# Masked level copies over the second halves only, and a ScalarE eviction moved behind the gate's first output

## The chip, the cores and the metric

The kernel runs on one core of a Trainium2 chip. The metric is the device time of one execution in microseconds. The engines are named as in the profile: PE is TensorE, DVE is VectorE, ACT is ScalarE, POOL is GpSimd, SP is SyncE, which here only issues DMAs. All data are fp32; a name with _r marks a tile that PE reads as fp32r.

## The reference, cut to what matters

Two transformer blocks over 256 tokens of width 1024. What the change touches is the first block's recurrent attention, its embedding gate, and the second block's gated linear attention; a mixture of experts ends the second block.

```python
def hgrn2_mix(q, f_logit, i_in, lb):          # first block, chunks of 64, 4 heads of 128
    ...
    diff = b[:, :, :, None, :] - b[:, :, None, :, :]
    decay = jnp.where(incl[:, :, None], jnp.exp(jnp.minimum(diff, 0.0)), 0.0)
    scores = jnp.einsum('bhtsk,bhsk->bhts', qb[:, :, :, None, :] * decay, kb)
    o_intra = jnp.einsum('bhts,bhsv->bhtv', scores, vb)

def first_block(...):
    ...
    mix = jnp.concatenate([o_hg, o_sb], axis=-1) @ w_out[i]
    h = h + rmsnorm(mix, attn_post_norm[i])
    ...
    h = h + rmsnorm(y, ffn_post_norm[i])
    h = h + (p[i] @ ple_proj[i]) * jax.nn.sigmoid(h @ ple_gate[i])

def gla_chunked(q, k, v, log_alpha):          # second block, 4 heads of 64
    ...
    scores = jnp.einsum("bnchd,bnshd->bnhcs", q_dec, k * jnp.exp(-b))
    causal = jnp.tril(jnp.ones((GLA_CHUNK, GLA_CHUNK), dtype=bool))
    scores = jnp.where(causal, scores, 0.0)
    o_intra = jnp.einsum("bnhcs,bnshe->bnche", scores, v32)

def hierarchical_moe(...):                    # 32 experts, 2 per token
    hid = jax.nn.silu(xb @ w_gate[e]) * (xb @ w_up[e])
    return hid @ w_down[e]
```

## The kernel before

Each engine has one program written out by hand; their order against each other is set by semaphores alone. `wait_ge(*upto("name", n))` waits until step n of that name is done, `.then_inc(sem("name"), 1)` marks one. `T` is 256 tokens, `TT` is 2 halves of `P` = 128.

*Levels of the first attention.* The causal scores are built from levels L = 1, 2, 4 .. 64 (`LEVELS`) and 128, in `ALL_LEVELS`. In a block of 2L tokens level L gives the scores of queries in its second half against keys in its first half. Four engines share each level:
- PE (L1526) multiplies whole 128x128 blocks for four heads and both token halves, 16 products into two banks, alternately banks 0, 1 and 2, 3. It waits for q and k of the level (`qk_ready`, `half_kept`) and until the copies two levels back have left the banks (`lv_out`).
- DVE takes the part of the products that belongs to the level: `collect` (L2083) issues two `copy_predicated` (L2091) of 128x512 from the banks into S4, under `lmask[:, mask, :]`, which is nonzero only where the query lies in the second half and the key in the first half of a block. The diagonal comes first, with mask DIAG; its products are L1511.
- DVE also makes the next level's q and k in `grow` (L2057): L2073 multiplies the second halves of q, L2076 the first halves of k, L2080 the totals, half as long at each level. For li from 2 on it waits for the products of two levels back; it also waits for ACT's halves.
- ACT copies the halves that don't change (L1107, L1110, `half_kept`) and after each of the first six levels makes a sixth of a softplus for the other attention (L1078 Abs, L1084 Exp, L1091 Ln over 128x1536, function `soft`, steps `sp`), with a table load ahead of Exp and of Ln.

Behind the last masked copy DVE makes 2 x 1536 columns of logs (L2106, waits for `sp` 6), copies level 128 plainly (L2111, 128x256 each), and then adds for eight heads (L2127), each released by PE's L1548 to L1551; ACT makes the Exp of each (L1123, `a_ready`). DVE goes on with the low parts of w_out's first chunks (L323).

*Weights in two parts.* A dense layer's weight chunk (1 MB raw, by DMA) is split by ACT into a high part (`act_hi`, L314, two casts of 128x1024) and by DVE into a low part (`dve_lo`, L323, two). `pe_chunk` then runs 48 matmuls of 256 columns (L385, L386, L387), and its last one marks `<layer>_done<j>`. Chunk (i, j) is round i in slot and bank j; round 1 of a slot needs the parts, which round 0's matmuls have read, and the bank, which round 0's output has left.

*The embedding gate.* PE's order is pp(0), the last down product, the norm, pp(1), gate chunk (0,0), pp(2), chunk (0,1), pp(3), chunk (1,0), chunk (1,1). pp(b) (L1655, 8 fp32 matmuls) is the embedding's product, alternately in banks 0 and 1; ACT evicts it in `pp_out` (L1193). pp(2) waits for pp_out(0) and pp(3) for pp_out(1). ACT's order is: casts of h for the gate (L362), pp_out(1) to pp_out(3), then for j in 0, 1 the wait for gate chunk (0, j), the high cast of chunk (1, j), `gate_out(0, j)` (L1210, a Sigmoid out of the bank, with a table load before the first). Then the high casts of proj2's first chunks, gate_out(1,0), squares of h3, gate_out(1,1). DVE's order is low (1,0), h3(0), low (1,1), h3(1), low of proj2 (0,0), h3(2), low of proj2 (0,1), h3(3). `h3(b)` (L2319, L2322) needs pp_out(b) and the gate's output of the same pair. Behind the chunks PE sums the adaptive products (L1688) and the norm's squares (L464); then the second block's projection proj2 starts. SP's later loads wait for `pgate_lo` and `proj2_lo`.

*The second attention.* `gla_collect` (L2407, copies at L2413) does for GLA what `collect` does: once with mask CHUNK (the causal chunks of 64), once with the mask of level 64; both copy 128x512 twice. PE's `gla_scores` come between proj2's chunks 4 to 7. DVE's steps around them are low casts of proj2 and the LRU's steps L2439 to L2449; L2447 waits for ACT's Tanh L1301.

*The end.* After routing, expert after expert runs (PE L1935 and L1958); SP loads 2 MB parts (L780) into three buffers, the first experts' ahead of the routing table on waits for `proj2_done`, `mix2_ready`, `wout2_done`, `nffn2_ss` and `xs_done`, the others as PE leaves a buffer.

Of the kernel before, what the change touches and what calls it, by code (L numbers as in the profile page):

```python
# [14 lines left out]
U32 = mybir.dt.uint32  # L15
# [4 lines left out]
P = 128  # L20
# [6 lines left out]
def build_program(nc, d, out):  # L27
# [16 lines left out]
    GLA_CHUNK = 64  # L44
    GATE_RANK = d["gla_wa2_2"].shape[1]
    GATE_NORM = 16.0
    LRU_C = 8.0
    NE, _, DE = d["w_gate_2"].shape[1:]
    NG = d["w_coarse_2"].shape[2]
    EPG = NE // NG  # L50
# [10 lines left out]
    with ctx:  # L61
        def sb(name, shape, dt=F32):
            return ctx.enter_context(nc.sbuf_tensor(name, shape, dt))
# [85 lines left out]
        def sem(name):  # L149
            name, _ = shared.get(name, (name, 0))  # L150
            if name not in sems:
                sems[name] = ctx.enter_context(nc.semaphore(name))
            return sems[name]
# [26 lines left out]
        S4 = sb("S4", [P, HT * T])  # L180
# [15 lines left out]
        LEVELS = [1, 2, 4, 8, 16, 32, 64]  # L196
        xs_at = -(-nc.sbuf_base // 32) * 32
        lmask = sb("lmask", [P, 9, P])
        DIAG, CHUNK = 7, 8
# [16 lines left out]
        VO, at = {}, 0  # L216
# [8 lines left out]
        bank = [ctx.enter_context(nc.psum_tensor(f"bank{i}", [P, 512], F32)) for i in range(4)]  # L225
# [3 lines left out]
        def tile(region, k, n=1):  # L229

            return region[:, k * T:(k + n) * T]
# [19 lines left out]
        def upto(name, value=1):  # L251

            _, before = shared.get(name, (name, 0))
            return sem(name), value + before
# [20 lines left out]
        def sp_load(sp, layer, i, j):  # L275
            name, w, _, sl = layer[:4]
            sp.dma_start(slot[sl[j]].rearrange("p (k n) -> p k n", k=KT),
                         w.rearrange("(k p) n -> p k n", p=P)[:, :, bass.ds(i * 512 + j * 256, 256)]
                         ).then_inc(sem(f"{name}_full{j}"), 16)
# [28 lines left out]
        def act_hi(act, layer, i, j):  # L308

            name, sl, parts = layer[0], layer[3], layer[4]  # L310
            act.wait_ge(*upto(f"{name}_full{j}", i * 16 + 16))
            for h in range(2):
                c = slice(h * HALF, (h + 1) * HALF)
                act.activation(slot_r[parts[2 * j]][:, c], slot[sl[j]][:, c], ACT.Copy  # L314
                               ).then_inc(sem(f"{name}_hi{j}"), 1)
# [42 lines left out]
        def act_source(act, name, src, at, ready):  # L358

            for b in range(4):  # L360
                ready(b)
                act.activation(tile(R24_r[:, at[0]:at[0] + KT * T], 2 * b, 2), tile(src, 2 * b, 2),  # L362
                               ACT.Copy).then_inc(sem(f"{name}_src_hi"), 1)
# [228 lines left out]
        def blocks(ap, L):  # L592
            return ap.rearrange("p (n l) -> p n l", l=2 * L)
# [405 lines left out]
        def _(act):  # L999
# [98 lines left out]
            for li in range(len(ALL_LEVELS) - 1):  # L1098
                L = ALL_LEVELS[li]
# [92 lines left out]
            def pp_out(b):  # L1192
                act.activation(tile(xk, 2 * b, 2), bank[PP_BANKS[b]][:, :], ACT.Copy  # L1193
                               ).then_inc(sem("pp_out"), 1)
# [7 lines left out]
            act_token_root(act, "nfpost", token_rms("nfpost"))  # L1202

            act_source(act, "pgate", hT, SRC_LO, lambda b: act.wait_ge(*upto("h2_ready", b + 1)))
            for b in range(1, 4):
                act.wait_ge(*upto("pp_done", b))
                pp_out(b)

            def gate_out(i, j):
                act.activation(tile(mixT, 4 * i + 2 * j, 2), bank[pgate[5][j]][:, :], ACT.Sigmoid  # L1210
                               ).then_inc(sem(f"pgate_out{j}"), 1)

            for j in range(2):
                act.wait_ge(*upto(f"pgate_done{j}", 1))
                act_hi(act, pgate, 1, j)
                gate_out(0, j)
            act_hi(act, proj2, 0, 0)
            act.wait_ge(*upto("pgate_done0", 2))
            gate_out(1, 0)
# [757 lines left out]
        def _(dve):  # L1977
# [105 lines left out]
            def collect(n, b0, mask):  # L2083

                dve.wait_ge(*upto("lv_done", n + 1))
                if n:

                    dve.wait_ge(*upto("lv_out", 2 * n))
                m = lmask[:, mask, :].bitcast(U32).unsqueeze(1).to_broadcast([P, 4, P])
                for b in range(2):  # L2090
                    dve.copy_predicated(  # L2091
                        S4[:, b * 512:(b + 1) * 512].rearrange("p (n t) -> p n t", t=P), m,
                        bank[b0 + b][:, :].rearrange("p (n t) -> p n t", t=P)
                    ).then_inc(sem("lv_out"), 1)

            dve.tensor_tensor(level_q(0), tile(projR, 0, 4), T4[:, :], ALU.mult
                              ).then_inc(sem("qk_ready"), 1)
            collect(0, 2, DIAG)
            for li in range(len(LEVELS)):
                grow(li)  # L2100
                collect(li + 1, 2 * (li % 2), li)
                if li == 6:
                    dve.wait_ge(*upto("sp", 6))
                    for n in range(2):
                        c = slice(n * 1536, (n + 1) * 1536)
                        dve.scalar_tensor_tensor(out=lb_[:, c], in0=zb[:, c], scalar=0.0, in1=lb_[:, c],  # L2106
                                                 op0=ALU.max, op1=ALU.add).then_inc(sem("lm_ready"), 1)
# [299 lines left out]
            def gla_collect(n, mask):  # L2407
                dve.wait_ge(*upto("gl_done", 2 * n + 2))
                if n:
                    dve.wait_ge(*upto("gl_out", 2 * n))  # L2410
                m = lmask[:, mask, :].bitcast(U32).unsqueeze(1).to_broadcast([P, 4, P])
                for b in range(2):
                    dve.copy_predicated(  # L2413
                        S4[:, b * 512:(b + 1) * 512].rearrange("p (n t) -> p n t", t=P), m,
                        bank[6 + b][:, :].rearrange("p (n t) -> p n t", t=P)
                    ).then_inc(sem("gl_out"), 1)

            def gla_qk(n, L):
# [11 lines left out]

            gla_qk(0, 64)
            gla_collect(0, CHUNK)
            dve_lo(dve, proj2, 3, 0)
            gla_qk(1, P)
# [6 lines left out]
            dve.wait_ge(*upto("lgate_out", 2 * HT))  # L2441
            dve.tensor_tensor(G4[:, :], G4[:, :], XC, ALU.mult).then_inc(sem("gi_ready"), 1)
            gla_collect(1, len(LEVELS) - 1)
            dve_lo(dve, proj2, 3, 1)
            dve.wait_ge(*upto("lru_a"))
# [344 lines left out]
```

## Time and profile before

| | us |
|---|---|
| median of 3 runs | 994.4 (994.0 to 994.59) |
| the profiled execution | 989.33 |
| its span | 987.6 |

| engine | busy us | share of the span |
|---|---|---|
| PE | 796.2 | 81% |
| PEld (weight loads of PE) | 655.7 | 66% |
| DVE | 486.1 | 49% |
| ACT | 355.9 | 36% |
| POOL | 51.5 | 5% |

How to read it: the shares are means over stages with different limits, so they don't say what a change in one stage is worth. The profile cuts the span into 40 slices of 24.7 us and gives a digit for each, the busy share in tenths. A timeline row begins with its start and its length; a row of x2 is two instructions in a row, and their lengths overlap a little, so the next start minus this start is what they cost the queue. Brackets at its end give the idle time before it and what ended that. In the chain of waits a piece is the part of an instruction that the end depended on.

### The profile page before, as it was taken

The page shows a single profiled execution, that of the slowest core. Times are in us where ns is not written, and L with a number is a line of the kernel's source. Part 1 is how long each engine was busy: PE and PEld are TensorE (multiplying, and loading weights), DVE is VectorE, ACT ScalarE, POOL GpSimd, SP SyncE. Part 2 cuts the span into 40 slices and gives each one's busy share as a digit, 9 for nine tenths or more (in the row PEclk, how much of TensorE's full clock was granted, in tenths as well). Part 3 has the DMA queues.
Part 4 walks back from the last instruction along what each step waited for, and adds up shares of the span by engine and source line. Part 5 has one row for each costly group of instructions (what it writes and reads, how often), then busy time and mean ns, then how long its engine had stood idle before and what let it go on. Part 6 is the DMA issues. An engine that isn't in the chain of part 4 may idle for free.

```text
span 987.6 us, 21230 instructions
## 1 busy us (share of the span) xinstructions
PE 796.2 (81%) x8283; PEld 655.7 (66%) x8284; DVE 486.1 (49%) x794; ACT 355.9 (36%) x488; POOL 51.5 (5%) x145
## 2 busy tenths in 40 slices
PE   5999889699999998879999998885575575685473
PEld 5999579699999998768989864543232332353241
DVE  3645687767787855375797543331221211331222
ACT  5432486364555644163885231110101101110102
POOL 4000100000000000001040000000000000000000
PEclk9999999899999999798999999998887988998877
DMA  7586322269898755343328767999999999999994
GB/s 269 178 281 241 110 84 88 86 250 339 294 313 294 261 187 185 103 152 106 109 69 330 288 257 285 422 429 425 424 430 425 423 430 426 423 430 425 424 428 167
DMA packets 89011, 278.77 MB, mean 282 GB/s; under 512 B 8031, under 2 KB 67850, under 8 KB 71562
## 3 DMA queue, kind: packets, MB, share of 16 engines
q1 hardware_dynamic: 88270, 276.86, 72.5%
q10 hardware_dynamic: 700, 1.36, 0.4%
q8 instruction: 27, 0.44, 0.2%
q14 instruction: 14, 0.11, 0.0%
HBM read 277.15 MB, written 1.05 MB: 282 GB/s over the span
## 4 chain that ended last, share of the span: by engine, by line
PE 54%; DMA 29%; DVE 9%; ACT 5%; issue 2%; SPq 0%; DVEq 0%; ACTq 0%
DMA projR<-in_w_up 20%; PE bank L385 10%; PE bank L387 9%; PE bank L386 9%; PE bank L1935 8%; DMA Whi<-in_w_up 7%; PE bank L1958 2%; DVE Whi_r L323 2%; PE acc L1632 1%; PE acc L1630 1%; PE acc L1627 1%; PE bank L1632 1%; PE bank L1630 1%; PE bank L1627 1%; ACT Whi_r L314 1%
## 5 line engine op out<-in xcount | busy, mean ns | idle before, releaser
L385 PE MATMUL bank<-R_r,Whi_r 128*128 128x256 f32 x800 | 234.7, 293 | 19.0 <-DVE R_r L2214 4.9
L386 PE MATMUL bank<-R_r,Whi_r 128*128 128x256 f32 x800 | 231.1, 289 | 0.0
L387 PE MATMUL bank<-R_r,Whi_r 128*128 128x256 f32 x720 | 207.1, 288 | 0.0
L385 PEld LDWEIGHTS bank<-R_r,Whi_r 128*128 128x128 f32 x800 | 158.4, 198 | 24.1 <-issue 13.7
L386 PEld LDWEIGHTS bank<-R_r,Whi_r 128*128 128x128 f32 x800 | 158.9, 199 | 0.1
L387 PEld LDWEIGHTS bank<-R_r,Whi_r 128*128 128x128 f32 x720 | 141.9, 197 | 0.0
L2717 DVE TENSOR_TENSOR V<-V,bank 64x256 f32<-64x256 f32 x34 | 14.4, 424 | 233.6 <-ACT V L1393 233.6
L1393 ACT ACTIVATE V<-bank 64x256 f32<-64x256 f32 x34 | 12.8, 376 | 217.6 <-PE bank L1935 217.6
L1935 PE MATMUL bank<-Whi,S 128*32 128x256 f32 x832 | 59.3, 448 | 37.1 <-DMA Whi<-in_w_up 32.3
L323 DVE TENSOR_TENSOR Whi_r<-Wlo,Whi_r 128x1024 fp32r<-128x1024 f32 x54 | 64.9, 1246 | 46.6 <-ACT Whi_r L314 46.5
L2159 DVE TENSOR_TENSOR Whi_r<-Wlo,Whi_r 128x2048 fp32r<-128x2048 f32 x33 | 75.6, 2289 | 24.7 <-ACT Whi_r L1179 11.7
L314 ACT ACTIVATE Whi_r<-Wlo 128x1024 fp32r<-128x1024 f32 x64 | 63.9, 1049 | 60.3 <-PE bank L387 59.4
L1935 PE MATMUL bank<-w_gate,S 128*32 128x256 f32 x352 | 52.8, 467 | 40.0 <-DMA projR<-in_w_up 37.7
L1935 PEld LDWEIGHTS bank<-Whi,S 128*32 128x32 f32 x832 | 29.8, 129 | 65.8 <-issue 54.5
L1935 PE MATMUL bank<-Wlo,S 128*32 128x256 f32 x640 | 46.6, 456 | 31.6 <-DMA Wlo<-in_w_up 28.1
L1935 PEld LDWEIGHTS bank<-w_gate,S 128*32 128x32 f32 x352 | 24.6, 133 | 55.7 <-issue 49.8
L1935 PEld LDWEIGHTS bank<-Wlo,S 128*32 128x32 f32 x640 | 23.7, 130 | 54.2 <-issue 46.3
L1935 PE MATMUL bank<-projR,S 128*32 128x256 f32 x352 | 53.6, 466 | 0.0
L1403 ACT ACTIVATE T_r<-SV 128x256 fp32r<-128x256 f32 x34 | 14.2, 416 | 87.5 <-DVE SV L2739 87.5
L2739 DVE SCALAR_TENSOR_TENSOR SV<-bank,small,pT 128x256 f32<-128x256 f32 x34 | 16.4, 484 | 43.2 <-PE bank L1958 43.2
L1935 PEld LDWEIGHTS bank<-projR,S 128*32 128x32 f32 x352 | 33.5, 133 | 1.9
L986 POOL COPY S<-projR 128x160 f32 x34 | 10.9, 321 | 390.8 <-PE bank L1935 362.4
(494 smaller groups left out, 1551.4 us busy)
## 6 DMA issues: line engine op xcount, KB each, us to landing
Wlo<-in_w_in SPq DMA_DIRECT2D x24, 1024.0 KB, 5.2
Wlo<-in_w_gate_up SPq DMA_DIRECT2D x22, 1024.0 KB, 5.1
Whi<-in_w_gate SPq DMA_DIRECT2D x10, 2048.0 KB, 31.1
Whi<-in_w_up SPq DMA_DIRECT2D x10, 2048.0 KB, 35.6
Whi<-in_w_down SPq DMA_DIRECT2D x10, 2048.0 KB, 37.3
Wlo<-in_w_gate SPq DMA_DIRECT2D x9, 2048.0 KB, 32.8
projR<-in_w_up SPq DMA_DIRECT2D x9, 2048.0 KB, 37.7
Wlo<-in_w_up SPq DMA_DIRECT2D x9, 2048.0 KB, 37.2
```

The costliest lines, as they stand in the source:

```text
L314: act.activation(slot_r[parts[2 * j]][:, c], slot[sl[j]][:, c], ACT.Copy).then_inc(sem(f"{name}_hi{j}"), 1)
L323: dve.tensor_tensor(slot_r[parts[2 * j + 1]][:, c], slot[sl[j]][:, c], slot_r[parts[2 * j]][:, c].bitcast(F32), ALU.subtract).then_inc(sem ...
L385: pe.matmul(o, w_hi[:, c], tile(x_hi, k), start=(k == 0), stop=False)
L386: pe.matmul(o, w_hi[:, c], tile(x_lo, k), start=False, stop=False)
L387: mm = pe.matmul(o, w_lo[:, c], tile(x_hi, k), start=False, stop=(k == KT - 1))
L1627: pe.matmul(o, slot_r[10][:, c], x_hi, start=(first and k == 0 and m % 2 == 0), stop=False, skip_group_check=True)
L1630: pe.matmul(o, slot_r[10][:, c], x_lo, start=False, stop=False, skip_group_check=True)
L1632: mm = pe.matmul(o, slot_r[11][:, c], x_hi, start=False, stop=(last and k == 1), skip_group_check=True)
L1935: mm = pe.matmul(bank[0][g * WIN:(g + 1) * WIN, 0:256], xw[:, k * WIN:(k + 1) * WIN], (gate, up)[g // 2][:, c:c + 256], start=(k == 0), st ...
L1958: mm = pe.matmul(bank[3][g * WIN:(g + 1) * WIN, 0:T], hidT[:, at:at + WIN], down[:, f * D + g * 256:f * D + (g + 1) * 256], start=(f == 0) ...
L2159: dve.tensor_tensor(dst, raw, hi.bitcast(F32), ALU.subtract).then_inc(sem(f"{name}_lo"), 1)
L2739: dve.scalar_tensor_tensor(out=yb, in0=bank[3][:, 0:T], scalar=wt_now, in1=gt2band, op0=ALU.mult, op1=ALU.mult).then_inc(sem("y_scaled"), 1)
```

## The change

Three edits. In `collect` the copies of all levels but the diagonal go only over the second half of each block of 2L columns: mask, source and destination are viewed as 4 x P/2L x L, 256 columns in place of 512. In `gla_collect` the copy under level 64's mask goes over columns 64 to 127 of each 128, with mask CHUNK it stays whole. The mask is zero in what is left out, so S4 is the same; PE's products stay whole. In the embedding gate ACT's pp_out(3) with its wait moves from before the loop over j into it, behind gate_out(0,0).

```diff
--- before.py
+++ after.py
@@ -1202,7 +1202,7 @@
             act_token_root(act, "nfpost", token_rms("nfpost"))
 
             act_source(act, "pgate", hT, SRC_LO, lambda b: act.wait_ge(*upto("h2_ready", b + 1)))
-            for b in range(1, 4):
+            for b in range(1, 3):
                 act.wait_ge(*upto("pp_done", b))
                 pp_out(b)
 
@@ -1214,6 +1214,9 @@
                 act.wait_ge(*upto(f"pgate_done{j}", 1))
                 act_hi(act, pgate, 1, j)
                 gate_out(0, j)
+                if j == 0:
+                    act.wait_ge(*upto("pp_done", 3))
+                    pp_out(3)
             act_hi(act, proj2, 0, 0)
             act.wait_ge(*upto("pgate_done0", 2))
             gate_out(1, 0)
@@ -2086,12 +2089,18 @@
                 if n:
 
                     dve.wait_ge(*upto("lv_out", 2 * n))
-                m = lmask[:, mask, :].bitcast(U32).unsqueeze(1).to_broadcast([P, 4, P])
                 for b in range(2):
-                    dve.copy_predicated(
-                        S4[:, b * 512:(b + 1) * 512].rearrange("p (n t) -> p n t", t=P), m,
-                        bank[b0 + b][:, :].rearrange("p (n t) -> p n t", t=P)
-                    ).then_inc(sem("lv_out"), 1)
+                    scores, new = S4[:, b * 512:(b + 1) * 512], bank[b0 + b][:, :]
+                    if mask == DIAG:
+                        m = lmask[:, mask, :].bitcast(U32).unsqueeze(1).to_broadcast([P, 4, P])
+                        scores, new = (a.rearrange("p (n t) -> p n t", t=P) for a in (scores, new))
+                    else:
+                        L = LEVELS[mask]
+                        m = blocks(lmask[:, mask, :], L)[:, :, L:2 * L].bitcast(U32).unsqueeze(1
+                            ).to_broadcast([P, 4, P // (2 * L), L])
+                        scores, new = (a.rearrange("p (m n l) -> p m n l", m=4, l=2 * L)[:, :, :, L:2 * L]
+                                       for a in (scores, new))
+                    dve.copy_predicated(scores, m, new).then_inc(sem("lv_out"), 1)
 
             dve.tensor_tensor(level_q(0), tile(projR, 0, 4), T4[:, :], ALU.mult
                               ).then_inc(sem("qk_ready"), 1)
@@ -2408,11 +2417,12 @@
                 dve.wait_ge(*upto("gl_done", 2 * n + 2))
                 if n:
                     dve.wait_ge(*upto("gl_out", 2 * n))
-                m = lmask[:, mask, :].bitcast(U32).unsqueeze(1).to_broadcast([P, 4, P])
+                at = 0 if mask == CHUNK else GLA_CHUNK
+                m = lmask[:, mask, at:P].bitcast(U32).unsqueeze(1).to_broadcast([P, 4, P - at])
                 for b in range(2):
                     dve.copy_predicated(
-                        S4[:, b * 512:(b + 1) * 512].rearrange("p (n t) -> p n t", t=P), m,
-                        bank[6 + b][:, :].rearrange("p (n t) -> p n t", t=P)
+                        S4[:, b * 512:(b + 1) * 512].rearrange("p (n t) -> p n t", t=P)[:, :, at:P], m,
+                        bank[6 + b][:, :].rearrange("p (n t) -> p n t", t=P)[:, :, at:P]
                     ).then_inc(sem("gl_out"), 1)
 
             def gla_qk(n, L):
```

## Rows read from the trace of the kernel before

**Rows 1.** The page: the slices' GB/s, and the chain that ended last

```profile
GB/s 269 178 281 241 110 84 88 86 250 339 294 313 294 261 187 185 103 152 106 109 69 330 288 257 285 422 429 425 424 430 425 423 430 426 423 430 425 424 428 167
...
PE 54%; DMA 29%; DVE 9%; ACT 5%; issue 2%; SPq 0%; DVEq 0%; ACTq 0%
```

**Rows 2.** The DMA queue's own waits: engine, line, waited for, us in total, times, longest

```profile
SPq L780 <- PE bank L1935: 162.3, 25, 17.1
```

**Rows 3.** Timeline of PE, 404 to 446: start us, us, line, operation, count, idle before

```profile
409.42 1.89 PE L1655 MATMUL bank<-pT,Wlo 128*128 128x256 f32 x8
...
416.91 1.89 PE L1655 MATMUL bank<-pT,Wlo 128*128 128x256 f32 x8
423.38 0.35 PE L385 MATMUL bank<-R_r,Whi_r 128*128 128x256 f32 x1 [4.58 <-ACT Whi L1210]
...
436.53 1.92 PE L1688 MATMUL bank<-projR,ones 128*32 128x512 f32 x16
```

**Rows 4.** Timeline of ACT, 404 to 424 us

```profile
411.35 0.60 ACT L1193 ACTIVATE R<-bank 128x512 f32<-128x512 f32 x1 [7.48 <-PE bank L1655]
418.84 0.60 ACT L1193 ACTIVATE R<-bank 128x512 f32<-128x512 f32 x1 [6.89 <-PE bank L1655]
419.33 1.99 ACT L314 ACTIVATE Whi_r<-Wlo 128x1024 fp32r<-128x1024 f32 x2
421.34 1.28 ACT L1210 ACT_TABLE_LOAD   x1
422.64 0.60 ACT L1210 ACTIVATE Whi<-bank 128x512 f32<-128x512 f32 x1
423.13 1.05 ACT L314 ACTIVATE Whi_r<-Wlo 128x1024 fp32r<-128x1024 f32 x1
```

**Rows 5.** Timeline of DVE, 404 to 446 us

```profile
420.41 2.36 DVE L323 TENSOR_TENSOR Whi_r<-Wlo,Whi_r 128x1024 fp32r<-128x1024 f32 x2 [16.30 <-ACT Whi_r L314]
```

**Rows 6.** Timeline of the DMA queue, 380 to 450 us: the gate's last two loads

```profile
388.14 2.64 SPq L277 DMA_DIRECT2D Wlo<-in_ple_gate  x2
```

**Rows 7.** The chain of waits in order of time, 384 to 446: start us, us, what

```profile
425.20 0.21 PE bank L386
...
430.97 0.12 PE bank L386
```

**Rows 8.** Timeline of DVE, 114 to 150 us (the levels)

```profile
119.18 0.68 DVE L2073 TENSOR_TENSOR R<-R,T 128x512 f32<-128x512 f32 x1
119.77 0.69 DVE L2076 TENSOR_TENSOR R<-projR,T 128x512 f32<-128x512 f32 x1
...
120.97 1.37 DVE L2091 COPY_PREDICATED S<-lmask,bank 128x512 f32<-128x512 uint32 x2
122.21 0.70 DVE L2073 TENSOR_TENSOR R<-R,rms 128x512 f32<-128x512 f32 x1
...
137.04 1.34 DVE L2091 COPY_PREDICATED S<-lmask,bank 128x512 f32<-128x512 uint32 x2 [0.47 <-PE bank L1526]
138.27 3.41 DVE L2106 SCALAR_TENSOR_TENSOR Whi<-Whi 128x1536 f32<-128x1536 f32 x2
141.61 0.74 DVE L2111 COPY SX<-bank 128x256 f32<-128x256 f32 x2
142.27 1.01 DVE L2127 TENSOR_TENSOR Whi<-acc,Whi 128x384 f32<-128x384 f32 x2
```

**Rows 9.** Timeline of ACT, 114 to 150 us

```profile
123.55 0.63 ACT L1107 ACTIVATE R<-R 128x512 f32<-128x512 f32 x1 [0.34 <-DVE R L2076]
...
134.27 0.61 ACT L1110 ACTIVATE R<-R 128x512 f32<-128x512 f32 x1
134.79 1.47 ACT L1091 ACTIVATE Whi<-Whi 128x1536 f32<-128x1536 f32 x1
```

**Rows 10.** Timeline of PE, 114 to 150 us

```profile
134.98 2.02 PE L1526 MATMUL bank<-R 128*128 128x128 f32 x16 [1.37 <-DVE R L2076]
```

**Rows 11.** Timeline of DVE, 446 to 550 us (second attention)

```profile
498.79 1.22 DVE L2447 TENSOR_TENSOR T<-mixin 128x1024 f32<-128x1024 f32 x1 [1.10 <-ACT projR L1301]
```

## The prediction

> **What bounds the kernel now.** The views were read from the whole to the stretch. The page first [rows 1]: the chain that ended last is 54% TensorE and 29% DMA. The slices show why: from slice 26 on (617 us) the DMA engines move about 425 GB/s without a break. That is the stream of expert weights, and nothing the change touches lies in it. Before it the DMA engines have room (257 to 330 GB/s in slices 22 to 25), and the queue's own waits say what the loads of experts wait for: L780 stood 162.3 us for TensorE's products [rows 2], hence for work, not for an absolute time. So whatever ends earlier ahead of the stream lets it start earlier by the same amount, and the end follows. What is left is to ask, for each of the three places, how much earlier its last wait ends. I took each engine's timeline there and laid them side by side.
>
> **Part 1: pp_out(3) moved (the embedding gate).** PE runs gate chunk (0,0), pp(2), chunk (0,1), pp(3), chunk (1,0), chunk (1,1). Between pp(3) (ends 418.81) and chunk (1,0) (starts 423.38) it idles 4.58 us for ACT's sigmoid L1210 [rows 3]. ACT is late for one reason: it evicts pp(2) at 411.35, then waits 6.89 us in L1193 for pp(3) [rows 4], though chunk (0,0), whose weights and bank it must free, was done when pp(2) began at 409.4. Behind that wait stand, on ACT, the two high casts of chunk (1,0) (L314, 1.99 us), the table load (1.28) and gate_out(0,0) (0.60); DVE's low casts, first at 420.41 after 16.30 idle us [rows 5]; and through both of them PE.
>
> With pp_out(3) behind gate_out(0,0) ACT goes on at 411.85: high casts to 413.8, table to 415.1, gate_out(0,0) to 415.7. DVE follows half a cast behind and has the low part by 415.2. The last weights of the gate were issued by 390.8 [rows 6], 21 us before the cast wants them. PE does not come to chunk (1,0) before 418.81, 3 us later, so its wait is gone: 4.5 us.
>
> The moved step's own cost: pp_out(3) now runs at 418.84 (0.5 us to the next start), between gate_out(0,0) and the casts of chunk (1,1). Queued behind its wait are act_hi(pgate,1,1), 419.33 to 421.3, DVE's low casts to 422.75, and gate_out(0,1), to 421.8. Chunk (1,1) wants them when chunk (1,0) ends, 418.9 + 48 x 0.12 = 424.7: 1.9 us of cover, so the step costs nothing on the path; without cover it would cost 0.5. A copy after a sigmoid shows no table load in this trace (L314 at 423.13 follows L1210 directly), so the swap adds none. DVE in that order: low casts (1,1) to 422.7, h3(1) to 424.1, low casts of proj2 (0,0) to 426.4, h3(2) to 427.8, low casts of proj2 (0,1) to 430.1; h3(3) wants it at 431.1, 1 us later. SP's waits on the same casts (loads of proj2's chunks 2 and 3, of wout2's first two) end earlier and meet an idle DMA.
>
> What is next late is PE itself. The two chunks took 423.38 to 436.53, 13.15 us; 96 matmuls at 0.12 would be 11.5. The rest is clock: 0.21 us each in a stretch of some 3 us round 425.2, 0.12 behind it [rows 7], that is the 1.2 GHz level just behind the idle gap and 2.4 GHz again after it. Chunk (0,1) before the gap ran at 0.12 all along. Without the gap I expect no low stretch: PE ends at 418.9 + 11.6 = 430.5 instead of 436.53. **Term: -6.0 us**, of it 4.5 for the wait, 1.5 for the clock; bounds 4.5 and 6.2. All that comes behind (gate_out(1,1), h3(3), the norm, proj2) hangs on the end of chunk (1,1).
>
> The Trainium skill (TensorE: Matmul & The Clock Gate, What's actually happening) says the array's clock is throttled by default and activity releases it; by that rule the low stretch goes with the gap. The trace agrees (low behind the gap, full before it). The same page says that the place of the switch in a burst varies from run to run; by that the sum would be 5.5 where an older low stretch slides into the new one.
>
> **Part 2: half copies in the first attention.** Eight collects of two copy_predicated each; the diagonal stays whole, seven levels halve: 14 copies of 256 instead of 512 elements. A pair takes 1.24 us of DVE's queue now (120.97 to 122.21) [rows 8], 0.62 each. No masked half copy is in the trace. The nearest rows are the plain copies of 256 out of PSUM, L2111: two from 141.61 to 142.27, 0.33 each. From below nothing shorter has a reason; from above, 0.62 (a stride that eats the gain). I take 0.36: 0.33 and the 0.03 by which a masked copy of 512 exceeds a product of 512 (0.59, from L2073 to L2076 at 119.18). Saved: 0.26 x 14 = 3.7 us of DVE.
>
> Most of that isn't on the path. A level costs DVE 1.24 + 0.60 + 0.60 + up to 0.34 for the totals, 2.5 to 2.8; but ACT has the kept halves (0.52 each, as from 134.27 to 134.79) and half a softplus step (1.4, as at 134.79) per level [rows 9], 2.5, and two table loads besides. Its last idle time is 0.34 us, ahead of 123.55 [rows 9]; from there to the end of its level work it has none. Product 6 starts at 134.98, 0.1 behind the end of ACT's L1110 (134.27 + 0.61), although the view names DVE's L2076 as the releaser [rows 9, 10]. So ACT is the floor. What comes through: (a) level 2's kept halves start when grow(1) is done; with one halved pair that is 0.53 earlier, ACT is free 0.43 earlier: 0.43, carried to product 6. (b) The last pair (137.04 to 138.27), straight on the path behind product 6 and ahead of L2106: 2 x 0.26 = 0.53. Together 0.96: DVE reaches L2127 at 141.3, not 142.27, and PE and DVE then hand the eight heads to each other as before. ACT's casts and table load ahead of the Exps move by 0.43 only, but a_ready has over 1 us of room before DVE's low casts of wout1 are over. **Term: -1.0 us**, bounds 0 and 1.5.
>
> The row for single elements, every other one, is L2073 at level 1: 0.68 us long, at level 2 0.70 [rows 8]; it reads SBUF, not PSUM. The Trainium skill (Vector Engine (DVE) Microarchitecture Reference, 5.2 Measured stream behaviour on trn2) speaks against this change at that level: a port runs at full rate only over runs of at least two adjacent words from an 8-byte boundary. An estimate by its table is 0.3 us for the pair of level 1, and the sum 6.7 for 7.0. L2073 doesn't agree with it.
>
> **Part 3: the half copy of the second attention.** Only gla_collect(1) halves; it saves 0.53. Behind it DVE casts, then waits 1.10 us for ACT's L1301 before L2447 [rows 11]: the 0.53 widens this wait. PE takes the scores behind it only after chunk 6, so its wait on gl_out isn't the last either. **Term: 0**, bounds 0 and 0.5.
>
> **Sum.** -6.0 - 1.0 - 0 = -7.0 us. The profiled execution took 989.33 us (span 987.6); it would take 982.3. The median of the runs shown is 994.4, 5.1 above it, and the stages that the change touches have no part in that; so the prediction is 994.4 - 7.0 = **987.4**, 0.7% faster.
>
> **Rivals.**
> 1. *The clock stays low.* Chunk (1,0) has its low stretch for another reason (a switch that comes late, some of ACT's waits left). Then only 4.5 + 1.0 are gained: 988.9. For it: levels switch elsewhere without a gap this long; against: chunk (0,1) at 0.12 throughout. Chance 0.15.
> 2. *The attention gives nothing*, the floor being ACT all through or the half copies as long as whole ones: 6.0 gained, 988.4. Against it: the pair at 137.04 has no ACT work beside it. Chance 0.12.
> 3. *More than forecast*, the shift moving another low stretch of the clock out of the way too: 985.9 for one as large as that of rows 7, 1.5 us. Chance 0.10.
> 4. *The gain is given back ahead of the stream*, some load of the first experts ending last: about 993.5. Against it: slices 22 to 25 well below 425 GB/s. Chance 0.03.
> 5. *Slower:* the strided masked copy. Place: DVE's queue in the levels, whose every copy is on the path once DVE falls behind ACT. Price: 14 x (d - 0.62), d a half copy's time. It outweighs part 1 by 2 us from d = 1.19 on; at 1.25 (twice a whole copy's) 8.8 us are lost, 6.0 gained: 997.2. Against it: L2073 at level 1. Chance 0.03.
>
> **How the numbers follow.** The forecast itself has 0.57. A measurement of this kernel can tell about 0.2%, 2 us, from no change. Faster by more: forecast and rivals 1 to 3, 0.94. Within: rival 4, 0.03. Slower: rival 5, 0.03. The range leaves out rivals 4 and 5 and holds 1 to 3 with both shortfalls together (989.9): 984.8 to 990.2.
>
> **What would show it.** Right: PE's gap before chunk (1,0) gone, the two chunks in 11.6 us, ACT's L1193 in front of the casts of (1,1) with no new table load; masked copies of 256 at some 0.36 each; ACT without idle time through the levels; L2106 some 1 us earlier after the diagonal copy; the wait before L2447 longer. Wrong: a PE gap before chunk (1,1); a wait of DVE on the casts of proj2 ahead of h3(3); masked copies over 0.6; or a first expert waiting for its weights.

## The result, and the profile after

The changed kernel took 984.19 us (median of 6 runs, 982.71 to 989.22), the kernel before 994.09 in the 6 runs beside it (990.01 to 994.59). The ratio is 0.993 with a 95% interval of 0.9906 to 0.9955: faster by 0.7%, which on the 994.4 of the forecast is 987.4, the predicted time. The bare median lies lower, 0.6 us under the predicted range (the quotient of the two medians is 0.990). The runs of the kernel before spread over 4.6 us here and those of the changed one over 6.5, and the section on the reasons comes back to that.

The profiled execution of the changed kernel was its slowest of the six: 989.22 us, span 987.5, against 989.33 and 987.6 before. Whoever compares only these two spans finds no gain. So the stages have to be laid side by side first. The page of the changed kernel shows the same shape as [rows 1]: the stream at about 425 GB/s now starts in the slice that it started in before.

```profile
GB/s 268 172 261 240 137 39 133 86 214 329 310 298 321 274 137 193 153 171 88 128 92 299 337 197 286 423 430 425 423 429 425 424 430 426 423 427 427 424 430 163
```

Stages, each measured between the starts of two named instructions in the profiled execution (lines are numbered as in the kernel before; in the other kernels the same code stands some lines further down. e1 to e11 are the experiments; e3 and e10 are the changed kernel again; in e5 and e11 the stretch from pp(3) to the row sums holds extra work. pp(2) to pp(3), 7.5 us in all, is left out):

| us | start to diagonal copy | diagonal copy to first L2127 | first L2127 to pp(2) | pp(3) to row sums | row sums to first gla copy | gla copy to first gate/up weights | those to the first down weights | to the stream | stream to store |
|---|---|---|---|---|---|---|---|---|---|
| before | 117.93 | 24.34 | 267.15 | 19.62 | 50.40 | 63.02 | 27.46 | 20.20 | 385.64 |
| after | 121.51 | 23.66 | 267.62 | 13.34 | 50.15 | 62.87 | 30.48 | 20.21 | 385.83 |
| e3 | 118.34 | 23.67 | 267.95 | 13.34 | 50.28 | 62.85 | 27.47 | 20.21 | 385.80 |
| e10 | 120.92 | 23.68 | 267.04 | 13.33 | 50.15 | 62.88 | 30.46 | 20.10 | 388.06 |
| e1 | 120.60 | 24.32 | 266.97 | 13.33 | 48.41 | 62.88 | 27.45 | 20.11 | 386.18 |
| e2 | 120.79 | 23.68 | 267.12 | 19.61 | 50.39 | 62.88 | 27.47 | 20.19 | 385.74 |
| e4 | 121.08 | 23.78 | 267.08 | 13.33 | 50.14 | 62.86 | 30.48 | 20.20 | 385.88 |
| e5 | 118.29 | 24.33 | 267.56 | 21.96 | 49.36 | 62.87 | 29.10 | 20.10 | 386.03 |
| e11 | 118.37 | 24.34 | 267.55 | 18.15 | 49.53 | 62.87 | 29.09 | 20.11 | 385.74 |

After against before: -0.68 in the levels and -6.28 in the gate, as the change means it; +3.58 in the first 118 us and +3.02 ahead of the first down weights, where not one instruction differs. These two cancel the gain in this one execution. e3, the same kernel with a span of 981.7, has neither of them.

What they are is seen in the windows of each kernel: first column the stretch, then its length and busy times; the third from the end is TensorE's granted clock as a share of 2.4 GHz. The third row of each is the whole stage ahead of the first down weights. Before:

```profile
13.00:30.00 17.00, 14.97 (x99) 14.40 (x100) 7.37 (x8) 10.38 (x18) 0.00 (x0) 0.90 0.53 186
104.00:122.00 18.00, 14.28 (x121) 10.94 (x118) 13.78 (x28) 8.56 (x13) 2.72 (x6) 1.00 0.37 118
549.95:577.41 27.46, 26.08 (x149) 21.96 (x149) 17.34 (x68) 11.78 (x21) 0.17 (x2) 0.94 0.97 395
```

After:

```profile
13.00:30.00 17.00, 14.77 (x86) 14.19 (x87) 6.01 (x6) 10.29 (x18) 0.00 (x0) 0.80 0.54 186
104.00:122.00 18.00, 15.11 (x115) 10.53 (x108) 10.95 (x23) 8.66 (x11) 2.72 (x6) 0.81 0.36 118
546.64:577.12 30.48, 29.04 (x149) 24.29 (x149) 17.34 (x68) 11.79 (x21) 0.16 (x2) 0.83 0.89 362
```

e3, the changed kernel again:

```profile
13.00:30.00 17.00, 14.89 (x96) 14.31 (x97) 7.05 (x7) 10.41 (x18) 0.00 (x0) 1.00 0.53 186
104.00:122.00 18.00, 14.27 (x121) 10.53 (x114) 13.78 (x29) 8.55 (x12) 2.72 (x6) 1.00 0.38 118
543.92:571.39 27.47, 26.11 (x149) 21.98 (x149) 17.35 (x68) 11.79 (x21) 0.17 (x2) 0.94 0.97 396
```

Where the instructions are the same, the long stretches are those with the lower granted clock. Ahead of the first down weights the same 149 matmuls stand in 27.46 us at 0.94, in 29.09 at 0.88 (e11) and in 30.48 at 0.83. In the first 122 us the changed kernel's profile has 0.80 and 0.81 in the two windows shown, where e3's has 1.00, and is 3.2 us longer. There the clock is not all of it: the kernel before has 0.90 in the first window and still reaches the diagonal copy 0.4 us sooner than e3, and five other kernels with the changed one's two shares (e1, e2, e4, e8, e10) need 120.60 to 121.08 us for its 121.51. The gain has to be read from the stages that the change touches.

**The gate.** Timeline of PE, changed kernel (start us, us, line, operation, count, idle before), which answers [rows 3]. Everything ahead is 3.37 us later than before, since pp(2) starts at 412.79 and not at 409.42:

```profile
412.79 1.89 PE L1658 MATMUL bank<-pT,Wlo 128*128 128x256 f32 x8
...
420.28 1.89 PE L1658 MATMUL bank<-pT,Wlo 128*128 128x256 f32 x8
421.82 0.47 PE L385 MATMUL bank<-R_r,Whi_r 128*128 128x256 f32 x1
422.13 0.28 PE L386 MATMUL bank<-R_r,Whi_r 128*128 128x256 f32 x1
...
433.62 1.92 PE L1691 MATMUL bank<-projR,ones 128*32 128x512 f32 x16
```

The idle time ahead of chunk (1,0) is gone, and in that listing all of the chunks' matmuls behind the first start 0.12 us apart. pp(3) to row sums went from 19.62 to 13.34, 6.28 less. The first matmul now starts under the tail of pp(3) and the second 0.31 behind it, so the split is read at the chunk's second matmul, 423.57 before and 422.13 now: 4.81 up to it (6.66 to 1.85), 1.47 from it to the row sums (12.96 to 11.49). Counted from the first matmul the chunks took 13.15 and take 11.80. ACT in the same stretch, for [rows 4]:

```profile
414.72 0.60 ACT L1193 ACTIVATE R<-bank 128x512 f32<-128x512 f32 x1 [7.48 <-PE bank L1658]
415.21 2.00 ACT L314 ACTIVATE Whi_r<-Wlo 128x1024 fp32r<-128x1024 f32 x2
417.23 1.28 ACT L1210 ACT_TABLE_LOAD   x1
418.53 0.60 ACT L1210 ACTIVATE Whi<-bank 128x512 f32<-128x512 f32 x1
422.21 0.60 ACT L1193 ACTIVATE R<-bank 128x512 f32<-128x512 f32 x1 [3.08 <-PE bank L1658]
422.70 2.00 ACT L314 ACTIVATE Whi_r<-Wlo 128x1024 fp32r<-128x1024 f32 x2
```

ACT still waits for pp(3), for 3.08 us, but nothing that PE needs soon stands behind that wait. No second table load appears between sigmoid and copy.

**The levels.** Timeline of DVE, changed kernel, for [rows 8]: the diagonal pair, the first halved pairs, and the last one:

```profile
121.51 1.35 DVE L2103 COPY_PREDICATED S<-lmask,bank 128x512 f32<-128x512 uint32 x2 [2.90 <-PE bank L1514]
...
124.56 1.30 DVE L2103 COPY_PREDICATED S<-lmask,bank 128x256 f32<-128x256 uint32 x2
125.66 0.72 DVE L2076 TENSOR_TENSOR R<-R,rms 128x512 f32<-128x512 f32 x1
...
129.78 0.75 DVE L2103 COPY_PREDICATED S<-lmask,bank 128x256 f32<-128x256 uint32 x2
130.45 0.67 DVE L2076 TENSOR_TENSOR R<-R,rms 128x512 f32<-128x512 f32 x1
...
140.50 0.78 DVE L2103 COPY_PREDICATED S<-lmask,bank 128x256 f32<-128x256 uint32 x2 [0.78 <-PE bank L1529]
141.17 3.42 DVE L2115 SCALAR_TENSOR_TENSOR Whi<-Whi 128x1536 f32<-128x1536 f32 x2
...
145.17 0.55 DVE L2136 TENSOR_TENSOR Whi<-acc,Whi 128x384 f32<-128x384 f32 x1
```

A pair's cost is read from start to next start. The halved pair of the third level and of all later ones takes 0.67 us (129.78 to 130.45), where a whole one took 1.24 before. At level 1 (runs of one element) it takes 1.10, and the same at level 2 (runs of two; 127.24 to 128.34).

**The second attention.** Timeline of DVE there, changed kernel, for [rows 11]:

```profile
490.91 0.79 DVE L2423 COPY_PREDICATED S<-lmask,acc 128x256 f32<-128x256 uint32 x2 [0.25 <-PE acc L1742]
...
495.63 1.23 DVE L2457 TENSOR_TENSOR T<-mixin 128x1024 f32<-128x1024 f32 x1 [1.69 <-ACT projR L1304]
```

The pair is shorter, and the wait behind it is wider by 0.59 us.

### The profile page after: what moved, and what is told of

It reads as the page before. It is cut to its first block, busy times and chain, and to the rows that moved or that the text cites. A ratio compares the mean times of both kernels' runs of the same rounds, so it can differ in the third digit from the quotient of the medians.

```text
span 987.5 us, 21230 instructions
## 1 busy us (share of the span) xinstructions
PE 800.3 (81%) x8283; PEld 659.3 (67%) x8284; DVE 483.1 (49%) x794; ACT 355.8 (36%) x488; POOL 52.0 (5%) x145
## 4 chain that ended last, share of the span: by engine, by line
PE 55%; DMA 29%; DVE 8%; ACT 5%; issue 2%; SPq 0%; DVEq 0%; ACTq 0%
DMA projR<-in_w_up 20%; PE bank L385 9%; PE bank L386 9%; PE bank L387 9%; PE bank L1938 8%; DMA Whi<-in_w_up 7%; PE bank L1961 2%; DVE Whi_r L323 2%; PE bank L1529 1%; PE acc L1635 1%; PE acc L1633 1%; PE acc L1630 1%; PE bank L1635 1%; PE bank L1633 1%; PE bank L1630 1%
```

## The experiments

The results of the extra matmuls and copies in e5, e11 and e8 are used by nothing.

**One part alone.** e1 is the kernel before with part 1 of the change (the eviction), e2 the kernel before with parts 2 and 3 (the copies). e3 is the changed kernel, unedited, on the same chip.

```
e1:  -            for b in range(1, 4):        # pp_out ahead of the chunk loop
     +            for b in range(1, 3):
     +                if j == 0:
     +                    act.wait_ge(*upto("pp_done", 3))
     +                    pp_out(3)
```

> Part 1 alone: ACT's eviction of pp(3) behind gate_out(0,0), all masked copies whole. My theory: from the start of pp(3) to the sums behind the gate's last chunk PE takes 13.3 us as in the changed kernel, not 19.6, so 6.0 to 6.3 us less, ratio 0.9938. Rival A (the clock's low stretch has nothing to do with the gap): 4.6 us less, the 96 matmuls of the two chunks 13.1 us, ratio 0.9954. Rival B (the time comes mostly from the attention): under 3 us less.

Measured: 986.86 us, ratio 0.994 (0.9919 to 0.9961), pp(3) to row sums 13.33, levels 24.32.

> Parts 2 and 3 alone: half copies in both attentions, ACT's order in the gate as before. My theory: ACT is the floor of the levels; from the diagonal copy to the first L2127 23.66 us as in the changed kernel's trace, not 24.34, so 0.7 us less and the ratio within noise of 1 (0.9993). Rival C (DVE's saved time is all on the path): 3.2 us less, 0.9968. Rival D (the changed order of clocks gives or takes more than the copies): over 2 us either way in the interval.

Measured: 991.77 us, ratio 0.9997 (0.998 to 1.0015), levels 23.68, gate 19.61.

> The changed kernel once more, for a second profile on this chip and for the sum. My theory: 6.3 + 0.7 = 7.0 us less, ratio 0.9930, and the stage durations (23.66 us for the levels, 13.34 for the gate) the same within 0.1 us in a second profile, whatever the low clock stretches elsewhere do. Rival E (the parts interact, or the first result's 9.9 us between the medians is the true size): 9 us less or more.

Measured: 983.42 us, ratio 0.9915 (0.9887 to 0.9943), both stages as in the first profile to 0.01. The intervals of e3 and of e10, further below, hold both 0.993 and 0.991, so whole runs don't decide on Rival E. The stages of this profile do: they hold 6.95 us between them, not 9.

The stages separate cleanly: each part moves its own and not the other's. Part 1 alone is measurably faster; parts 2 and 3 alone are not, as 0.7 us is less than the runs can tell; e2's interval excludes Rival C's 0.9968.

**Is the gate's second 1.5 us the clock?** The idle gap went, and so did the late casts; either could be why the chunks run in 11.80 and not 13.15. e5 keeps the order of the kernel before and fills PE's gap with matmuls on tiles that nobody reads; e11 has half as many.

```
             (behind the then_inc of pp(3), kernel before)
+            for n in range(5):
+                for k in range(PLE // P * 2):        # e11: range(2)
+                    pe.matmul(bank[4][:, (k % 2) * T:(k % 2 + 1) * T], ident[:, :],
+                              slot[5][:, k * T:(k + 1) * T], start=True, stop=True)
```

> The kernel before with 20 further matmuls (128x256 fp32, 0.217 us each, 4.3 us, results unused, into a free bank) between pp(3) and chunk (1,0), where PE idles 4.58 us. ACT is as late as before, so the wait itself stays. My theory (the low stretch is the price of the gap): the 96 matmuls of the two chunks then run at 0.12 us from the first on, 11.6 us in place of 13.15, and the kernel is 1.5 us faster for doing more: ratio 0.9985. Rival A (the low stretch lies there for another reason): 13.1 us again, ratio 1.000.

Measured: 993.54 us, ratio 1.0009 (0.9993 to 1.0024). Timeline of PE, e5:

```profile
417.67 1.89 PE L1655 MATMUL bank<-pT,Wlo 128*128 128x256 f32 x8
419.40 8.80 PE L1683 MATMUL acc<-Wlo,ident 128*128 128x256 f32 x40
427.85 0.47 PE L385 MATMUL bank<-R_r,Whi_r 128*128 128x256 f32 x1
...
439.63 1.92 PE L1692 MATMUL bank<-projR,ones 128*32 128x512 f32 x16
```

The twenty matmuls stand in the trace as 40 of 0.21 us each, so the filling is 8.45 us long and not 4.3. That is more than the gap, it delays chunk (1,0), and the whole kernel doesn't get the 1.5 us that was expected. But the chunks take 11.78 us, with ACT's sigmoid as late behind pp(3) as it was.

> The kernel before with 10 further fp32 matmuls of 256 columns between pp(3) and chunk (1,0). In e5 twenty of them were two passes each, 40 in all, and took 8.45 us, 3.9 more than the gap; ten should take 4.3 and end about when ACT's sigmoid does. My theory (the clock's low stretch is the price of the gap): the two chunks take 11.5 to 11.8 us and not 13.15, from the start of pp(3) to the sums 18.3 us and not 19.62: 1.3 us less for more work. Rival A: 13.1 us for the chunks, 19.7 for the stage. The unprofiled runs can't tell 1.3 us from none.

Measured: 989.73 us, ratio 0.9975 (0.9955 to 0.9995). Timeline of PE, e11:

```profile
419.48 4.48 PE L1683 MATMUL acc<-Wlo,ident 128*128 128x256 f32 x20
424.22 0.36 PE L385 MATMUL bank<-R_r,Whi_r 128*128 128x256 f32 x1 [0.26 <-ACT Whi L1210]
...
435.90 1.92 PE L1692 MATMUL bank<-projR,ones 128*32 128x512 f32 x16
```

Here chunk (1,0) starts 6.47 us behind pp(3), released by ACT's sigmoid, as in the kernel before, and the chunks take 11.68 us; from the second matmul on 11.49, as in the changed kernel. The granted clock behind the start of the chunk, in the kernel before and in e11:

```profile
424.10:427.50 3.40, 3.40 (x18) 3.40 (x18) 3.40 (x4) 3.40 (x5) 0.00 (x0) 0.51 0.02 5
424.90:428.50 3.60, 3.60 (x33) 3.60 (x32) 3.56 (x4) 3.45 (x5) 0.00 (x0) 1.00 0.00 0
```

The kernel does ten more matmuls than before, all of them useless, and its stage is 1.47 us shorter (18.15 for 19.62); its whole runs are 0.25% faster, just clear of none. The casts of chunk (1,1) run beside the chunks here as they did before, so it wasn't they. The 1.5 us were the clock behind the idle gap: shown. Rival 1 falls.

**What do short runs cost?** e4 is the changed kernel with levels 1 and 2 copied whole again.

```
-                    if mask == DIAG:
+                    if mask in (DIAG, 0, 1):
```

> The changed kernel with levels 1 and 2 copied whole, half copies from level 4 on. In the changed kernel's trace a pair of half copies took 1.10 us at levels 1 and 2, 0.67 from level 4 on, a whole pair 1.24. My theory: the levels lose only what level 1's pair gave ACT's start, 0.1 us, so from the diagonal copy to the first L2127 23.8 us. Rival G (the slow copies of levels 1 and 2 hold up the path by more than their length): no change, or a gain, from leaving them whole.

Measured: 988.37 us (one run, beside one of 991.01 of the kernel before); diagonal copy to L2127 23.78, and the last masked pair starts 19.11 behind the diagonal copy, exactly as before the change. So the halves at levels 1 and 2 are worth 0.1 us together, through pairs that are 0.14 shorter each; the last pair gives 0.56. Rival G falls.

e8 is the kernel before with pairs of masked copies of 256 elements (and two pairs of plain ones) put on DVE ahead of the gate's casts, with the run length, the source's memory or the one contiguous operand varied:

```
+            for n in range(2): ... dve.copy_predicated(*masked(n, 1, ps)).then_inc(...)          # L2335
+            for n in range(2): ... dve.copy_predicated(*masked(n, 1, ps, ('dst',))).then_inc(...) # L2345
     (and so on: run length 1, 2, 4, 8, 64; source PSUM or SBUF; mask, source or dst contiguous)
```

> The kernel before with 32 further masked copies in pairs on DVE while it idles ahead of the gate's second casts (results unused). They measure a copy of 256 columns by itself. From PSUM, all three operands stepping in blocks of L: levels 1, 2, 4, 8, 64; from SBUF: 1, 2, 4; from PSUM with only the mask, the source or the destination contiguous, at levels 1 and 2; plain copies at 1 and 2. Theory S (single words are slow on every port, pairs are not; then level 2 would be fast): 0.55 at level 1 and 0.33 at level 2. Theory P (the slow port is PSUM's, for runs under 4 words): 0.55 at levels 1 and 2 from PSUM, 0.33 from SBUF, and 0.33 with the source contiguous. Theory M (it is the mask, stepping inside a repeated dimension): 0.33 with the mask contiguous, and plain copies at 0.33.

Measured: 993.87 us (one run). Timeline of DVE, e8. L2335 to L2339: source in PSUM, all operands in runs of 1, 2, 4, 8, 64. L2340 to L2342: source in SBUF, runs of 1, 2, 4. L2343 to L2345: runs of 1 with the mask, the source, the destination contiguous. L2346 to L2348: the same for runs of 2. L2349: plain copy, runs of 1.

```profile
408.51 1.32 DVE L2335 COPY_PREDICATED T<-lmask,acc 128x256 f32<-128x256 uint32 x2
409.86 1.33 DVE L2336 COPY_PREDICATED T<-lmask,acc 128x256 f32<-128x256 uint32 x2
411.22 0.76 DVE L2337 COPY_PREDICATED T<-lmask,acc 128x256 f32<-128x256 uint32 x2
...
413.62 1.33 DVE L2340 COPY_PREDICATED T<-lmask,G 128x256 f32<-128x256 uint32 x2
...
416.35 0.78 DVE L2342 COPY_PREDICATED T<-lmask,G 128x256 f32<-128x256 uint32 x2
417.15 1.33 DVE L2343 COPY_PREDICATED T<-lmask,acc 128x256 f32<-128x256 uint32 x2
418.52 1.33 DVE L2344 COPY_PREDICATED T<-lmask,acc 128x256 f32<-128x256 uint32 x2
419.88 0.78 DVE L2345 COPY_PREDICATED T<-lmask,acc 128x256 f32<-128x256 uint32 x2
420.69 1.30 DVE L2346 COPY_PREDICATED T<-lmask,acc 128x256 f32<-128x256 uint32 x2
422.02 1.30 DVE L2347 COPY_PREDICATED T<-lmask,acc 128x256 f32<-128x256 uint32 x2
423.36 0.78 DVE L2348 COPY_PREDICATED T<-lmask,acc 128x256 f32<-128x256 uint32 x2
424.17 0.76 DVE L2349 COPY T<-acc 128x256 f32<-128x256 f32 x2
```

None of the three theories holds: runs of two are as slow as single elements (against S), the source may lie in PSUM or SBUF (against P), and a contiguous mask or source changes nothing (against M). Of what was tried, only a contiguous destination, or runs of at least four, brings a pair from 1.33 to 0.78 us; what in the engine makes it so, no run shows. A plain copy with the same destination in single elements shows nothing of it.

e8 also says something on the gap. The copies held up DVE's casts, so PE idled 6.32 us ahead of chunk (1,0), and the chunks took 14.01 us (0.50 granted from 428.00 to 433.00): a longer gap cost more behind it than the 4.58 us did.

**Who is the floor in the levels?** The forecast names ACT. e6 is the kernel before, e7 the changed one, with ACT's softplus steps taken out of the levels and put behind them:

```
-                if li < 6:
-                    soft(li)
             (behind the loop over the levels)
+            for n in range(6):
+                soft(n)
```

> The kernel before, with the six softplus steps of ACT behind all levels instead of one behind each. It takes ACT's floor out of the levels; L2106 and all behind it come later, so only the levels are read: from the start of the diagonal copies (L2091) to the start of the last masked pair. Both theories: DVE-bound, about 2.5 us per level, 18.5 to 19.1 us as before.

> The changed kernel with the softplus steps behind the levels, beside e6. My theory (ACT was the floor): without it the half copies show in full: each level from 8 on needs DVE 0.67 + 1.2 + 0.17 = 2.05 us and PE 2.0, so the levels take 3.0 us less than in e6, where in the changed kernel they took 0.1 less than in the one before. Rival F (PE's products and their round trip with DVE are the floor, not ACT): under 1 us less than e6.

Measured: 999.58 and 993.63 us (one run each; the moved steps now lie on the path). Diagonal copy to last masked pair: 18.53 in e6 (117.89 to 136.42), 16.42 in e7 (120.30 to 136.72). With ACT out of the way the same change of the copies is worth 2.1 us up to that pair, with ACT in it 0.1. ACT held the kernel before by only 0.6 us (19.11 to 18.53), as DVE was close behind it; it holds the changed one by 2.6 (19.00 to 16.42). Timeline of PE, e7:

```profile
125.80 2.05 PE L1529 MATMUL bank<-R 128*128 128x128 f32 x16 [0.88 <-DVE R L2079]
128.47 9.36 PE L1529 MATMUL bank<-R 128*128 128x128 f32 x72 [0.61 <-DVE R L2079]
```

I had expected 3.0; from the product at 128.47 on PE has no idle time left and is the next floor. Rival F (under 1 us) falls.

**A version that uses it.** e9 is the changed kernel with the softplus steps put where ACT waits anyway: two behind the first kept halves, and so on.

```
-                if li < 6:
-                    soft(li)
+                for n in {0: (0, 1), 1: (2,), 2: (3,), 3: (4,), 6: (5,)}.get(li, ()):
+                    soft(n)
     (lam's Exp stands behind its Abs; ahead of L2106's first half DVE waits for five steps, not six)
```

> The changed kernel with the floor that is left moved: ACT's softplus steps 0 and 1 (and the table load for Exp) in its idle time behind level 1's halves, steps 2 to 4 behind the next three levels, step 5 behind the last; L2106's first half waits only for step 5 of 6. My theory (ACT is the floor, e6 and e7): from the diagonal copy to the first L2127 22.0 us and not 23.67, the last masked pair 1.6 us earlier; 0.2% faster than the changed kernel. Rival F (PE and DVE hold the levels where they are): 23.6 us.

> The changed kernel a third time, on the same chip as e9, for the comparison and for the size of the whole effect: ratio 0.993 by the sum of the parts (6.3 + 0.7 us); Rival E: 0.991 again, as in e3, then the parts' stages don't hold all of it.

Measured, on one chip: e9 985.44 us, ratio 0.9924 (0.9895 to 0.9954); the changed kernel (e10) 986.44, ratio 0.9926 (0.9899 to 0.9953). Timeline of DVE, e9:

```profile
118.26 1.37 DVE L2102 COPY_PREDICATED S<-lmask,bank 128x512 f32<-128x512 uint32 x2 [2.71 <-PE bank L1513]
...
135.47 0.77 DVE L2102 COPY_PREDICATED S<-lmask,bank 128x256 f32<-128x256 uint32 x2
...
140.13 1.06 DVE L2135 TENSOR_TENSOR Whi<-acc,Whi 128x384 f32<-128x384 f32 x2
```

The levels take 21.87 us (118.26 to 140.13) where the changed kernel has 23.66: 1.8 us less, and all of it stands ahead of the last masked pair (135.47, 17.21 us behind the diagonal copy, for 19.00), so it comes from ACT's order. One execution of e9 took 978.9 us, the shortest of this study, but the two ratios do not differ: by whole runs e9 is not shown to beat the changed kernel.

## Why the prediction was right, and where it was not

**The gate: right, by its own steps.** Shifted by 3.37 us, its times can be laid on the trace: gate_out(0,0) over at 419.1 (forecast 415.7, so 419.07), pp_out(3) at 422.21 (418.84, so 422.21), the row sums at 433.62 (430.5, so 433.87); h3(3) on DVE waited 1.08 us for its sigmoid where 1 was forecast. Term 6.28 for 6.0: the wait gave 4.81 (forecast 4.5), the clock 1.47 (1.5). The chunks' second matmul starts where the forecast had their first, at 418.76 shifted back for 418.9, and they take 11.49 from there for the 11.6 assumed. e11 shows the split: with the wait left in and the gap filled the stage is 1.47 shorter. The upper bound of 6.2 was 0.1 too low. The Trainium skill (TensorE: Matmul & The Clock Gate, What's actually happening) has the throttled clock as the default that activity releases; the runs agree, since the chunks take 13.15 us behind 4.58 idle ones, with 0.51 granted in the low stretch, and 11.68 and 11.78 when PE is kept busy ahead of them. The sum of 5.5 us that its rule of the varying place left open came in none of the seven profiles that have part 1: 13.33 or 13.34 us from pp(3) to the row sums in each.

**The first attention: right in kind, too large by 0.3.** Forecast 0.96, measured 0.68. Part (b), the last pair, is right: 0.57 (1.24 to 0.67) for 0.53. Part (a) was mis-sized: 0.43 forecast, 0.12 measured. The step that failed is "with one halved pair that is 0.53 earlier": it priced every half copy at 0.36, while at level 1 each takes 0.55, and the pair is 0.14 shorter, not 0.53. The timeline of ACT, changed kernel, shows the rest of the step to be right; its wait ahead of level 2's kept halves is this row, for [rows 9]:

```profile
127.01 0.63 ACT L1107 ACTIVATE R<-R 128x512 f32<-128x512 f32 x1 [0.24 <-DVE R L2079]
```

It starts 5.50 us behind the diagonal copy, against 5.62 before (123.55 less 117.93): 0.12 earlier, which arrives undiminished at the last product. What misled was the row chosen for the stride, L2073: at level 1 it reads and writes SBUF at every other element and takes 0.59 us for 512 columns, for 0.60 at the later levels, but it is not a masked copy. The rule of the Trainium skill (Vector Engine (DVE) Microarchitecture Reference, 5.2 Measured stream behaviour on trn2) warned of single words, and I set it aside because L2073 did not agree. It came out at level 1 (an estimate of 0.3 us for the pair by its table; measured 0.43 above the later levels) and by it the term would have been 0.7, as measured. It did not come out at level 2, where by the page pairs of words run at full rate and the pair takes the same 1.10 us, nor for a single-word mask, source or plain copy (e8). That ACT is the floor is shown by e6, e7 and e9.

**The second attention: right.** 0.59 us more of waiting, for 0.53 forecast, and no gain from it: the stretch from the first gla copy to the first weights is 62.88 us in e2 and in e1, which has no part 3 (63.02 before).

**The sum and the run.** Measured stages: -6.28 and -0.68, -6.96 for -7.0. That the sum fits to 0.04 is luck: the gate gave 0.28 more than forecast and the levels 0.28 less. The stages between passed it on whole: e3's profile is 5.9 us below that of before (981.7 for 987.6), its touched stages 6.9 below, and the rest is 0.4 and 0.8 us more in the first two untouched stretches. So rival 4 (given back) fell; rival 2 fell too, as the levels gave 0.7; rival 5's price was never near 1.19, since 0.55 is still under 0.62. Rival 3, that the shift also moves other low stretches, can't be settled: over all runs of the changed kernel here (20) the mean is 985.3 and the median 983.7, over all of before (51) 992.7 and 992.8. The means differ by 7.5, near the stages' 7.0; the medians by about 9. The runs of both kernels lie in groups (13 of the 20 from 982.7 to 984.9, most others from 988.0 to 990.2; 20 of the 51 from 989.4 to 991.3, the others up to 998.0), so a median of few runs jumps between them. Whether the change makes the lower group likelier, or 20 runs are too few, stays open. My base of 994.4, from three runs, lay in the upper group: from 992.8 the same sum gives 985.8.

## What to carry to other kernels

Look on each engine for a wait that stands in front of work which does not need it: moving one eviction behind one activation gave nine tenths of this gain, and the gap that it closed had cost a third more than its length (1.47 on 4.58 us), because TensorE's clock fell for a stretch just behind it. Halving an operation pays only where its engine is the floor: the 2.6 us that DVE saved ahead of the last pair (four pairs at 0.57, two at 0.14) were worth 0.1, and a change of ACT's order then gave 1.8. Compare stages, not spans, where untouched code varies by more than the change is worth.

## What the runs showed of the hardware that was not expected

- A masked copy of 128x256 elements takes 0.335 us of DVE's queue when its destination comes in runs of four words or more or is contiguous, and 0.55 when it comes in runs of one or two (starts in the changed kernel; in e8 a pair lasts 1.33 us for 0.78, its end included). With the destination contiguous, source and mask in runs of one or two cost nothing (0.78), nor does a destination of single elements in a plain copy (0.76).
- TensorE's granted clock in identical code differs between executions, and a place is worth 2 to 4 us. The stretch ahead of the first down weights takes 26.60 us at a share of 1.00 (e8), 27.46 at 0.94, 29.09 at 0.88 and 30.48 at 0.83; the one behind the row sums 48.41 at 0.96 (e1) and 50.40 at 0.93 (before), though 49.02 at 0.97 in e8. The first 118 us take 118.3 to 118.4 where both windows above have 1.00 (e3, e5, e9, e11) and 120.6 to 121.5 where they have 0.80 and 0.81.
- Not every such difference is the clock. The stream's tail takes 388.06 us in e10 at a granted 0.87, but 386.03 in e5 at 0.86; the cause of the 2 us stays open.
- Useless matmuls in an idle gap made the stage shorter (e11): the chunks behind them took 11.68 us for 13.15, the whole kernel 0.9975 of the time (0.9955 to 0.9995). Behind a longer gap, 6.32 us, they took 14.01 (e8).
